# Stage route: place decoding on GpSimd, gates formed behind the second search, tiles written out

## What is computed

```python
qry = (hb @ w_query).reshape(t, P_HEADS, 2, P_HALF)
s = jnp.einsum('thcd,hckd->thck', qry, sub_keys).astype(jnp.float32)
top_s, top_i = lax.top_k(s, P_TOPK)
cand_s = (top_s[:, :, 0, :, None] + top_s[:, :, 1, None, :]).reshape(t, P_HEADS, P_TOPK * P_TOPK)
cand_i = (top_i[:, :, 0, :, None] * P_KEYS + top_i[:, :, 1, None, :]).reshape(t, P_HEADS, P_TOPK * P_TOPK)
best_s, best_pos = lax.top_k(cand_s, P_TOPK)
expert = jnp.take_along_axis(cand_i, best_pos, axis=-1)
gate = jax.nn.softmax(best_s, axis=-1)
```

## Time and profile before

| | us |
|---|---|
| median of 3 runs | 3873.57 |
| lowest and highest | 3871.1, 3877.83 |
| the profiled execution | 3871.7 |
| its span | 3869.9 |
| busy: PE, DVE, ACT, POOL | 3343.5, 2667.2, 1084.9, 1622.4 |
| stage route in the span | 1148.6 to 1574.7 |

### The profile page before, as it was taken

One profiled execution on the slowest core, in us unless ns is written; L12 is line 12 of the kernel. 1 busy time (PEld: TensorE's weight loads), 2 busy tenths in 40 slices (PEclk: granted clock), 3 DMA queues, 4 the chain that ended last, 5 costly groups with the idle time before them and its releaser, 6 DMA issues.

```text
span 3869.9 us, 49782 instructions
## 1 busy us (share of the span) xinstructions
PE 3343.5 (86%) x17534; PEld 2831.2 (73%) x17534; DVE 2667.2 (69%) x5420; ACT 1084.9 (28%) x1628; POOL 1622.4 (42%) x1283
## 2 busy tenths in 40 slices
PE   7999996999979981466299998998999999999999
PEld 6888874566539871465288887888888888888888
DVE  3000004444324999899288998998988899899998
ACT  3111112333311110599122222222222222222221
POOL 0000005323100000000367777777777687777775
PEclk9999997999989995799599999999999999999999
DMA  3222215222222000155988998999988899999997
GB/s 134 93 92 92 92 60 214 93 96 77 91 89 95 16 5 7 41 161 159 328 307 309 334 329 314 335 330 332 336 312 323 316 347 353 337 358 348 343 347 278
DMA packets 338429, 833.98 MB, mean 216 GB/s; under 512 B 25856, under 2 KB 128640, under 8 KB 337024
## 3 DMA queue, kind: packets, MB, share of 16 engines
q0 software_dynamic: 129024, 469.82, 33.1%
q1 hardware_dynamic: 180768, 323.26, 24.8%
q10 hardware_dynamic: 28512, 39.52, 2.8%
HBM read 743.71 MB, written 88.80 MB: 215 GB/s over the span
## 4 chain that ended last, share of the span: by engine, by line
PE 23%; DVE 15%; POOL 7%; issue 5%; DMA 1%; ACT 0%; ACTq 0%; DVEq 0%; SPq 0%
PE exp_vp L1870 12%; PE exp_up L1853 11%; DVE exp_ring L1788 5%; DVE exp_now L1795 4%; POOL exp_ring L1618 4%; DVE exp_acc L1766 3%; DVE exp_am_lo L1757 2%; POOL exp_v_lo L1609 2%; POOL exp_u_lo L1604 1%; DMA exp_u_raw<-in_u 1%; DVE exp_pr L1752 1%; DMA exp_acc<-scratch_h2T 0%; ACT exp_am_hi L1673 0%; DVE exp_now L1791 0%; DVE exp_dot L1788 0%
## 5 line engine op out<-in xcount | busy, mean ns | idle before, releaser
L1853 PE MATMUL exp_up<-exp_h_hi,exp_u_hi 128*128 128x320 f32 x2048 | 637.5, 311 | 54.9 <-POOL exp_u_lo L1604 54.9
L1618 POOL DMA_INDIRECT exp_ring<-in_u_rows,exp_eid x448 | 425.1, 949 | 565.7 <-DMA exp_eid<-scratch_eid 300.8
L1870 PE MATMUL exp_vp<-exp_v_hi,exp_am_hi 128*128 128x512 f32 x1280 | 515.0, 402 | 145.3 <-POOL exp_v_lo L1609 65.9
L1853 PE MATMUL exp_up<-exp_h_lo,exp_u_hi 128*128 128x320 f32 x2048 | 637.8, 311 | 0.0
L1853 PE MATMUL exp_up<-exp_h_hi,exp_u_lo 128*128 128x320 f32 x2048 | 637.7, 311 | 0.0
L1795 DVE SCALAR_TENSOR_TENSOR exp_now<-exp_ring,exp_dot,exp_now 128x1024 f32<-128x1024 f32 x444 | 569.9, 1284 | 15.9 <-DVE exp_now L1795 0.9
L1766 DVE TENSOR_TENSOR exp_acc<-exp_acc,exp_vp 128x512 f32<-128x512 f32 x640 | 435.5, 681 | 169.0 <-PE exp_vp L1870 155.5
L1788 DVE CUSTOM_DVE_ANT_0 exp_ring<-exp_now,exp_ring 128x1024 f32<-128x1024 f32 x448 | 533.5, 1213 | 1.0 <-ACT exp_now L1730 1.0
L1618 POOL DMA_INDIRECT exp_ring<-in_v,exp_eid x448 | 424.5, 948 | 217.6 <-DVE exp_now L1795 112.5
L1870 PE MATMUL exp_vp<-exp_v_hi,exp_am_lo 128*128 128x512 f32 x1280 | 510.2, 399 | 0.0
L1870 PE MATMUL exp_vp<-exp_v_lo,exp_am_hi 128*128 128x512 f32 x1280 | 505.1, 395 | 0.0
(11 more groups left out here) (202 smaller groups left out, 5267.1 us busy)
## 6 DMA issues: line engine op xcount, KB each, us to landing
exp_u_raw<-in_u SPq DMA_DIRECT2D x128, 512.0 KB
exp_v_raw<-in_v SPq DMA_DIRECT2D x128, 512.0 KB
scratch_gates<-spr_g SPq DMA_DIRECT2D x5, 8192.0 KB
exp_gt<-scratch_gates SPq DMA_DIRECT2D x128, 320.0 KB
scratch_z<-prj_zo ACTq DMA_DIRECT2D x33, 768.0 KB, 3.5
prj_w_raw<-in_w_in SPq DMA_DIRECT2D x44, 512.0 KB, 4.2
mix_zg<-scratch_z SPq DMA_DIRECT2D x9, 1024.0 KB
rt_wq<-in_w_q SPq DMA_DIRECT2D x4, 2048.0 KB, 15.0
```

The costliest lines, as they stand in the source:

```text
L1618: nc.gpsimd.indirect_dma_start(out=ring[:, n % RING, :], out_offset=None, in_=d["u_rows"] if n < PICKS else d["v"], in_offset=bass.Indirec ...
L1853: last = nc.tensor.matmul(up[:, g, 0:GW], u[a][:, o, k * P:(k + 1) * P], h2[b][:, k, cols(g)], start=(k == 0 and n == 0), stop=(k == KD - ...
L1870: last = nc.tensor.matmul(vp[:, bank, :], am[b][:, 1 - half, o, t * P:t * P + P], v[a][:, 2 * (1 - half) + o, c], start=(o == 0 and n == 0 ...
```

## The change

- The products and folds of the decoding (`decode`) and the last add, now L1121 to L1132, are GpSimd's; VectorE keeps the two `hit` rows (now L1291). A new semaphore `decoded` says that `out`'s first two rows stand.
- The expert numbers (`numbers`, L1299) and the gates of tile t-1 (L1309 to L1313) are formed in tile t between the second search and the candidates.
- VectorE waits for the products of tile t-1 before it writes `tf`, and for its decoding before it writes `hit`.
- TensorE's turn waits for gates and decoding.
- All nine tiles are written out.

```diff
...
@@ -1112,6 +1112,28 @@
             nc.gpsimd.iota(iota16[:, :], [[1, TOPK]], base=0, channel_multiplier=0,
                            allow_small_or_imprecise_dtypes=True).then_inc(iota_set, 1)
 
+            def decode(t):
+
+                for c in range(2):
+                    pool.wait_ge(hit_ready, 2 * t + c + 1)
+                    pool.wait_ge(keyed, 2 * t + c + 1)
+                    h4 = hit[:, c, :, :].rearrange("p a (k h) -> p a k h", h=PH)
+                    nc.gpsimd.tensor_tensor(h4, h4, tf[:, c, :, :].rearrange("p a (o h) -> p a o h", o=1)
+                                            .broadcast_to([P, TOPK, TOPK, PH]), ALU.mult).then_inc(picked, 1)
+                pool.wait_ge(picked, 2 * t + 2)
+                for n, rows in enumerate((8, 4, 2)):
+                    nc.gpsimd.tensor_tensor(hit[:, :, 0:rows, :], hit[:, :, 0:rows, :], hit[:, :, rows:2 * rows, :], ALU.add
+                                            ).then_inc(folded, 1)
+                    pool.wait_ge(folded, 3 * t + n + 1)
+                if t <= NS + 1:
+                    after(pool, eid_ready, t)
+                if t > NS:
+                    pool.wait_ge(out_turned, t - NS + 1)
+                nc.gpsimd.tensor_tensor(out[:, 0:2, :], hit[:, :, 0, :], hit[:, :, 1, :], ALU.add).then_inc(decoded, 1)
+
+            for t in range(NT):
+                decode(t)
+
         @block.scalar
         def _(act):
             act.sem_inc(stored, 16)
@@ -1130,7 +1152,7 @@
                 if t <= NS:
                     act.wait_ge(eid_ready, t + 1)
                     act.dma_start(d["eid"][t, :, :], eid[:, :]).then_inc(kept, 16)
-                    act.wait_ge(out_ready, 2 * t + 2)
+                    act.wait_ge(out_ready, t + 1)
                     act.dma_start(d["gate"][t, :, :], out[:, 2, :]).then_inc(kept, 16)
                 if t < NS:
                     return
@@ -1177,8 +1199,6 @@
                 take_wait()
                 for h in range(HC):
                     V.max(tv[:, h // 2, h % 2, 0:8], sc[:, u, h, :]).then_inc(top8, 1)
-                if not first:
-                    gates(t - 1)
                 dve.wait_ge(top8, HC * t + HC)
                 take_wait()
                 for h in range(HC):
@@ -1195,12 +1215,17 @@
                 take_wait()
                 for h in range(HC):
                     V.max_index(ti[:, h // 2, h % 2, 8:16], tv[:, h // 2, h % 2, 8:16], sc[:, u, h, :]).then_inc(found16, 1)
+                if isinstance(t, int) and 1 <= t <= NS + 1:
+                    numbers(t - 1)
+                if not first:
+                    gates(t - 1)
                 for p0, a0, rows, w in COVER:
                     V.tensor_tensor(cand[:, :, p0:p0 + rows * w].rearrange("p h (a b) -> p h a b", a=rows),
                                     tv[:, :, 0, a0:a0 + rows].rearrange("p h (a o) -> p h a o", o=1).broadcast_to([P, PH, rows, w]),
                                     tv[:, :, 1, 0:w].rearrange("p h (o b) -> p h o b", o=1).broadcast_to([P, PH, rows, w]),
                                     ALU.add).then_inc(cand_ready, 1)
                 dve.wait_ge(found16, HC * t + HC + GT * HC)
+                after(dve, picked, 2 * t)
                 for c in range(2):
                     V.tensor_copy(tf[:, c, :, :], ti[:, :, c, :].rearrange("p h a -> p a h")).then_inc(keyed, 1)
                 dve.wait_ge(cand_ready, len(COVER) * (t + 1))
@@ -1259,37 +1284,27 @@
                 dve.wait_ge(b_done, 6 * t + 5)
                 V.tensor_tensor(ab[:, 1, :, :], place[:, 2, :, :], row[:, 2, :, :], ALU.subtract).then_inc(b_done, 1)
 
+                after(dve, decoded, t)
                 for c in range(2):
                     if c == 1:
                         dve.wait_ge(b_done, 6 * t + 6)
                     V.tensor_tensor(hit[:, c, :, :], places[:, :, :],
                                     ab[:, c, :, :].rearrange("p k h -> p (k h)").rearrange("p (o s) -> p o s", o=1)
                                     .broadcast_to([P, TOPK, SLOTS]), ALU.is_equal).then_inc(hit_ready, 1)
-                for c in range(2):
-                    dve.wait_ge(hit_ready, 2 * t + c + 1)
-                    dve.wait_ge(keyed, 2 * t + c + 1)
-                    h4 = hit[:, c, :, :].rearrange("p a (k h) -> p a k h", h=PH)
-                    V.tensor_tensor(h4, h4, tf[:, c, :, :].rearrange("p a (o h) -> p a o h", o=1).broadcast_to([P, TOPK, TOPK, PH]),
-                                    ALU.mult).then_inc(picked, 1)
-                dve.wait_ge(picked, 2 * t + 2)
-                V.tensor_tensor(hit[:, :, 0:8, :], hit[:, :, 0:8, :], hit[:, :, 8:16, :], ALU.add).then_inc(folded, 1)
-                dve.wait_ge(folded, 3 * t + 1)
-                V.tensor_tensor(hit[:, :, 0:4, :], hit[:, :, 0:4, :], hit[:, :, 4:8, :], ALU.add).then_inc(folded, 1)
-                dve.wait_ge(folded, 3 * t + 2)
-                V.tensor_tensor(hit[:, :, 0:2, :], hit[:, :, 0:2, :], hit[:, :, 2:4, :], ALU.add).then_inc(folded, 1)
+
+            def numbers(t):
+
+                dve.wait_ge(decoded, t + 1)
+                after(dve, kept, 32 * t)
+                V.scalar_tensor_tensor(out=eid[:, :], in0=out[:, 0, :], scalar=float(PK), in1=out[:, 1, :],
+                                       op0=ALU.mult, op1=ALU.add).then_inc(eid_ready, 1)
+
+            def gates(t):
+
                 if isinstance(t, int) and t <= NS + 1:
                     after(dve, kept, 32 * t)
                 if not isinstance(t, int) or t > NS:
                     dve.wait_ge(out_turned, t - NS + 1)
-                dve.wait_ge(folded, 3 * t + 3)
-                V.tensor_tensor(out[:, 0:2, :], hit[:, :, 0, :], hit[:, :, 1, :], ALU.add).then_inc(out_ready, 1)
-                if isinstance(t, int) and t <= NS:
-                    dve.wait_ge(out_ready, 2 * t + 1)
-                    V.scalar_tensor_tensor(out=eid[:, :], in0=out[:, 0, :], scalar=float(PK), in1=out[:, 1, :],
-                                           op0=ALU.mult, op1=ALU.add).then_inc(eid_ready, 1)
-
-            def gates(t):
-
                 dve.wait_ge(expd, t + 1)
                 V.tensor_reduce(den[:, 0, :], shift[:, :, :], AX.X, ALU.add).then_inc(summed, 1)
                 dve.wait_ge(summed, t + 1)
@@ -1299,12 +1314,8 @@
                                 den[:, 1, :].rearrange("p (h o) -> p h o", o=1).broadcast_to([P, PH, TOPK]), ALU.mult).then_inc(out_ready, 1)
 
             tile(0, 0, first=True)
-            for t in range(1, NS + 1):
+            for t in range(1, NT):
                 tile(t, t % 2)
-            tile(NS + 1, (NS + 1) % 2)
-            with dve.Fori((NS + 1) // 2, NT // 2) as pair:
-                tile(2 * pair + 1, 1)
-                tile(2 * pair + 2, 0)
             gates(NT - 1)
 
         @block.tensor
@@ -1340,7 +1351,8 @@
             def turn(t):
                 if t < NS:
                     return
-                pe.wait_ge(out_ready, 2 * t + 2)
+                pe.wait_ge(out_ready, t + 1)
+                pe.wait_ge(decoded, t + 1)
                 after(pe, outT_ready, t - NS)
                 for c in range(3):
                     last = nc.tensor.transpose(tp[:, c * P:(c + 1) * P], out[:, c, :], ident[:, :])
```

More of the change, by code:

```diff
@@ L1087, in route @@
             top8 found8 cut8 top16 found16 keyed cand_ready best8 bfound8 bcut8 best16 bfound16
-            split placed a_done b_done hit_ready picked folded tables shifted expd summed recip out_ready out_turned outT_ready stored eid_ready kept""".split()
+            split placed a_done b_done hit_ready picked folded tables shifted expd summed recip out_ready out_turned outT_ready stored eid_ready kept decoded""".split()
         (const_in, w_in0, w_in1, w_in2, w_in3, h2_in0, h2_in1, iota_set, q_ready, q_out, s_ready, s_out,
          top8, found8, cut8, top16, found16, keyed, cand_ready, best8, bfound8, bcut8, best16, bfound16,
-         split, placed, a_done, b_done, hit_ready, picked, folded, tables, shifted, expd, summed, recip, out_ready, out_turned, outT_ready, stored, eid_ready, kept
+         split, placed, a_done, b_done, hit_ready, picked, folded, tables, shifted, expd, summed, recip, out_ready, out_turned, outT_ready, stored, eid_ready, kept, decoded
          ) = [s.sem(n) for n in names]
```

## The result

The changed kernel takes **3847.52 us** (median of 4 runs, 3845.48 to 3849.51); the kernel before, timed beside it, 3875.7 us (4 runs, 3871.1 to 3879.47). The ratio is 0.9928, with a 95% interval of 0.9911 to 0.9945: 0.7% faster, and clear of the noise. The profiled execution took 3849.51 us, its span 3847.7. The forecast was 3847 us, faster.

A forecast was written before the change was run, and what follows sets the result against it. VectorE was taken to set the length of the third stage, with GpSimd free. Terms -37.0 - 2.7 + 0.8 + 12.3 = -26.6 us, set against the median 3873.6, gave 3847 us; range 3837 to 3860.

The forecast's parts named there:

- Tile 0 is worth 0: Taking tile 0's decoding, about 5.3 us, off VectorE gains nothing, since tile 1 starts when its scores are there.
- Tiles 1 to 7, -37.0: Decoding off VectorE in tiles 1 to 7 saves 7 x 5.28 = 37.0 us if GpSimd is ready in time.
- the jump, -2.7: Writing out the VectorE loop removes its one jump back, between tiles 6 and 7: 2.7 us saved.
- gates, +0.8: Moving the gates from behind the first search to behind the second costs +0.8 us in all.
- Gates +0.1 us a tile: The per-tile price of moving the gates behind the second search, from steps between dependent VectorE rows: +0.1 us.
- Tile 8 pays 12.3: Last tile: no next tile covers GpSimd's decoding, taken as 18.4 us, so the stage ends 12.3 us later.
- The wait at the numbers: Rival: decoding over 19.2 us delays the expert numbers, each us costing 3; 0.14 together with TensorE's pace, still faster.
- The rival of held searches: GpSimd rows hold VectorE's searches in tiles 2 to 8, up to 129 us, 3976; 0.07 together with decoding above 26.
- the quicker GpSimd: Rival: GpSimd is quicker on 16-bit elements, decoding 9.5 us, only tile 8 changes, 3838 us; chance 0.20.
- The rival of TensorE as the pace: ScalarE's hold makes tiles 3 to 6 take 37 us, not 34: 12 us, 3859; 0.14 together with the numbers' wait.
- The total: Whole kernel: 3873.6 - 26.6 = 3847 us, with measurement able to tell about 0.2%, 7.7 us.

The follow-up runs named there:

- Experiment 1: Changed kernel with the place decoding back on VectorE for all nine tiles, gates, numbers and written-out tiles kept: 3870.86 us, ratio 0.9997 to the kernel before.
- experiment 2: Changed kernel with the gates back behind the first search, decoding still on GpSimd: 3868.65 us, ratio 0.9987 to the kernel before.
- Experiment 6: Changed kernel with GpSimd's first product waiting for both hit rows instead of one: 3859.81 us, timed only once.
- experiment 4: Changed kernel with two further GpSimd products a tile into a spare tile that nothing reads: 3881.31 us, ratio 1.0019 to the kernel before.

## Why the prediction was right

*Tile 0 is worth 0*: right. Tile 1 starts 58.7 us behind tile 0 in both profiles, and the idle time ahead of it is 25.4 us, forecast 25.

*Tiles 1 to 7, -37.0; the jump, -2.7; gates, +0.8; together -38.9*: measured -38.8. Experiment 1 separates the parts. The decoding back on VectorE costs 5.16 us a tile (39.37 against 34.21), so seven tiles gain 36.1 and not 37.0, and the jump and the new places together are worth 2.7, not 1.9. That the sum fits to 0.1 us is in part luck: the two errors cancel.

*Gates +0.1 us a tile*: the number is right (39.44 - 5.28 + 0.1 = 34.26 and 39.14 - 5.28 + 0.1 = 33.96 by the prediction's terms, 34.21 and 34.01 measured), the reasoning had a hole. I compared two places by the steps between dependent rows, as if GpSimd were silent, though two paragraphs on I used to say that two-input rows disturb each other. The gate product is such a row. In the old place it costs 3.26 us a tile and takes back 22.6 of 29.3 us (experiment 2). The move is thus no side piece: most of the gain hangs on it, and that it was right where it stood is luck as far as the prediction goes. Since GpSimd is done 15.5 us into a tile and the product comes at 20.0 (1342.54 - 1322.54), there are 4.5 us of margin.

*Tile 8 pays 12.3*: it paid 9.5. This is the mis-sized term, and it is all of the difference between -26.6 and -29.3. Two assumptions failed. The first is the duration: 2.1 ns an element from f32 rows, where the folds give (4.061 - 2.120)/1024 = 1.9 ns in bf16, and an undisturbed product with a broadcast operand takes 3.64 us. The second is that GpSimd starts when the second hit row ends; it started with the first one's end and paid 0.92 us for the overlap. Experiment 6 tells them apart. With the start as I assumed it the decoding takes 1541.40 - 1525.83 = 15.6 us instead of 18.4, which is the whole error; the earlier start gains only 16.89 - 16.66 = 0.2. The duration also rested on a misread row: 1.260 us (L547) is not the least for 512 elements with two inputs. The kernel before has such a product at 1.04 us, with a broadcast operand too (lines, min/median/max ns):

```profile
L560 POOL TENSOR_TENSOR mix_rot<-mix_rot,mix_k_dec x9: 1038/1039/1045, 612.9 to 1052.1; 128x512 f32<-128x512 f32 x9
```

Whether 16-bit elements or the shape of the operands makes the rows cheaper, no run tells.

*The wait at the numbers*: none, as forecast, with 1341.80 - 1338.04 = 3.8 us to spare instead of 0.8 (GpSimd's last add of tile 2 ends at 1338.04). That each us over the limit costs three us holds too: experiment 4 has three waits of 4.45 us, 13.3 in all.

*The rival of held searches*: false, and for the reason given against it. The searches' lines of the changed kernel (min/median/max ns):

```profile
L1201 DVE MAX8 rt_tv<-rt_sc x144: 271/275/295, 1195.4 to 1495.9; 128x8 f32<-128x128 f32 x144
...
L1205 DVE FIND_INDEX8 rt_ti<-rt_tv,rt_sc x144: 283/285/288, 1198.7 to 1500.2; 128x8 uint32<-128x128 f32 x144
```

Both stand beside GpSimd's rows in tiles 2 to 8 and alone in tiles 0 and 1, and minimum and maximum are 24 and 5 ns apart; the first search's maximum was 295 ns before the change too. *The rival of TensorE as the pace* is false too: seven tiles in a row take 34 us. Of the quicker GpSimd a third came true: 15.6 us instead of 18.4, not 9.5.

*The total*: 3873.6 - 29.3 would be 3844; measured 3847.5 and 3851.9, which is 28.2 and 26.7 us below the kernel before as timed beside each. That 3847.52 meets the forecast of 3847 to half a microsecond is luck: the sum was 2.7 us short, and the kernel before came out 2.1 us higher than the median I started from. The total confirms no more than the 0.2% named.

## What to carry to other kernels

Work that costs three times as much on an idle engine can still pay when the busy one sets the length. Count it on the path only where nothing of a next round covers it, here the last tile, and give that one back to the fast engine. When GpSimd is given two-input work, list VectorE's own two-input rows and place them outside of GpSimd's window: a row of 0.39 us in the wrong place can wait for a whole GpSimd instruction, and the profile shows this as its duration, not as idle time. After each gain look for the hole that it widened: the 25 us ahead of tile 1 were worth nearly as much as the change itself.

## What the runs showed that I had not expected

A two-input VectorE row that starts beside a running GpSimd instruction ends only behind it: 0.39 us became 3.27, 3.46 and 3.77, and each of the three ended some 0.24 us behind the end of the GpSimd instruction. GpSimd's product is held likewise by VectorE's second hit row, for 0.92 us. The searches for maxima and for indices, the reductions and the reciprocals beside the same GpSimd rows were no longer than without them. And TensorE's queries with 128 columns cost hardly more a column than with 256: 28.75 us for one tile, where a group of two took 55.4, both at a granted clock of 1.00.
